# Expert weights of a mixture-of-experts decoder step: 12 loads of 1 MB per expert become 6 of 2 MB, with strided transposes

## The reference

```
logits = x @ router_w + router_b                      # 32 experts, top 4 per token
gate   = softmax(top 4 logits)
for each expert e, for its tokens:
    h      = x @ w_gu[e] + b_gu[e]                    # 1024 -> 2048
    hg, hu = h[:, :1024], h[:, 1024:]
    act    = (clip(hu, -7, 7) + 1) * min(hg, 7) * sigmoid(1.702 * min(hg, 7))
    y     += gate * (act @ w_down[e] + b_down[e])     # 1024 -> 1024
```

## Time and profile before

| | us |
|---|---|
| median of 3 runs (1538.61 to 1538.96) | 1538.8 |
| the profiled execution | 1540.0 |
| its span, first to last instruction | 1538.0 |
| TensorE busy (9323 matmuls) | 1448.0 |
| VectorE busy | 523.0 |
| ScalarE busy | 287.9 |

### The profile page before, as it was taken

One profiled execution on the slowest core, in us unless ns is written; L12 is line 12 of the kernel. 1 busy time (PEld: TensorE's weight loads), 2 busy tenths in 40 slices (PEclk: granted clock), 3 DMA queues, 4 the chain that ended last, 5 costly groups with the idle time before them and its releaser, 6 DMA issues.

```text
span 1538.0 us, 24574 instructions
## 1 busy us (share of the span) xinstructions
PE 1448.0 (94%) x9323; PEld 684.9 (45%) x9323; DVE 523.0 (34%) x1106; ACT 287.9 (19%) x501; POOL 107.4 (7%) x174
## 2 busy tenths in 40 slices
PE   6978899999999989999999999999999999999995
PEld 4755568866665633333333333333333333333332
DVE  6877665442321142321321322312131223122223
ACT  3111331212213321111111111111111111111111
POOL 1189600000000000000000000000000000000000
PEclk9998899997999989999999999999999999999997
DMA  7853111012658549999999999999999999999991
GB/s 308 178 126 56 52 62 57 30 57 100 272 206 363 202 158 418 417 419 418 416 418 419 418 416 418 419 417 418 418 418 416 418 419 418 417 418 419 416 383 46
DMA packets 86697, 471.61 MB, mean 307 GB/s; under 512 B 7986, under 2 KB 13234, under 8 KB 46964
## 3 DMA queue, kind: packets, MB, share of 16 engines
q1 hardware_dynamic: 80356, 460.90, 74.0%
q10 hardware_dynamic: 6288, 9.95, 3.3%
HBM read 465.08 MB, written 5.74 MB: 306 GB/s over the span
## 4 chain that ended last, share of the span: by engine, by line
PE 60%; DMA 15%; SPq 13%; DVE 5%; issue 4%; ACT 2%; DVEq 0%; ACTq 0%
DMA big<-in_w_gu 15%; PE bank L1009 14%; SPq L529 10%; PE bank L586 10%; PE bank L1039 10%; PE bank L959 4%; SPq L515 3%; PE bank L669 2%; PE bank L1058 2%; PE bank L839 2%; PE bank L763 1%; PE bank L965 1%; PE bank L973 1%; ACT big L1293 1%; PE bank L755 1%
## 5 line engine op out<-in xcount | busy, mean ns | idle before, releaser
L1009 PE MATMUL bank<-big 128*64 128x512 f32 x2048 | 456.0, 597 | 16.3 <-DMA big<-in_w_gu 16.3
L1009 PEld LDWEIGHTS bank<-big 128*64 128x64 f32 x2048 | 141.2, 137 | 317.2 <-issue 257.8
L1039 PE MATMUL bank<-big 128*64 128x512 f32 x1024 | 226.8, 595 | 0.0
L1851 DVE TENSOR_TENSOR big<-big,bank 128x320 f32<-128x320 f32 x256 | 104.7, 483 | 355.1 <-PE bank L1058 355.1
L586 PE MATMUL bank<-big 128*128 128x320 f32 (+1 forms) x688 | 189.0, 434 | 2.3 <-ACT big L1238 1.3
L586 PEld LDWEIGHTS bank<-big 128*128 128x128 f32 x688 | 132.7, 194 | 57.9 <-issue 6.5
L1837 DVE TENSOR_SCALAR big<-bank 128x512 f32<-128x512 f32 x32 | 22.2, 693 | 331.5 <-PE bank L1009 331.5
L1039 PEld LDWEIGHTS bank<-big 128*64 128x64 f32 x1024 | 70.8, 137 | 133.2 <-issue 127.8
L1307 ACT ACTIVATE big<-big 128x512 f32<-128x512 f32 x32 | 20.3, 633 | 525.1 <-DVE big L1837 525.1
L1091 ACT ACTIVATE big<-bank 128x320 f32<-128x320 f32 (+3 forms) x122 | 53.2, 436 | 250.4 <-PE bank L586 59.1
L959 PE MATMUL bank<-big 128*64 128x512 f32 x396 | 94.2, 611 | 0.2 <-issue 0.2
(11 more groups left out here) (357 smaller groups left out, 1217.7 us busy)
## 6 DMA issues: line engine op xcount, KB each, us to landing
big<-in_w_gu SPq DMA_DIRECT2D x256, 1024.0 KB, 18.9
big<-in_w_down SPq DMA_DIRECT2D x128, 1024.0 KB, 21.9
big<-in_dense SPq DMA_DIRECT2D x47, 1024.0 KB, 7.9
big<-u_windows ACTq DMA_DIRECT2D x32, 160.0 KB, 7.3
out_y<-big SPq DMA_DIRECT2D x3, 512.0 KB, 2.7
big<-in_smw SPq DMA_DIRECT2D x1, 1408.0 KB, 19.4
big<-in_xT SPq DMA_DIRECT2D x2, 640.0 KB, 4.6
big<-in_b_gu SPq DMA_DIRECT2D x66, 4.0 KB
```

What stands on the lines that cost most here:

```text
L1009: last = mm(ps[bank][part, :], xte[:, k, :], w[:, at:at + 512], start=False, stop=(k == KT - 1))
L1039: last = mm(ps[4][part, :], actT[:, k % 4, (k // 4) * CAP:(k // 4 + 1) * CAP], w[:, k % 2, s * 512:s * 512 + 512], start=(k == 0), stop=(k ...
L1851: tt(part, part, ps[bank][:, 0:T], add).then_inc(psum_free[bank], 1)
```

## The change

Two chunks become one load. Load j (0 to 3) of `w_gu` takes 256 consecutive rows, and partition p gets rows 2p and 2p+1 of them, 16 KB that are consecutive in memory. Load 4 or 5, of `w_down`, takes 512 rows, and partition p gets rows 4p to 4p+3, 16 KB too. The slots are the same, taken in neighbouring pairs. Since a partition now holds rows 2p and 2p+1 instead of p and 128 + p, the transposes read every second column of `hrow` and every fourth of `hact`, so that the contraction meets the right rows. TensorE waits once per load, and tells SyncE once per load that it is used (`load_used`).

```diff
@@ -111,6 +111,10 @@
 USES = [SLOT.count(s) for s in range(SLOTS)]
 NTH = [SLOT[:c].count(SLOT[c]) for c in range(NPRE)]
 EXPERT_CHUNKS = 12
+LOADS = EXPERT_CHUNKS // 2
+LOAD_SLOT = [EXPERT_SLOT[2 * j] for j in range(LOADS)]
+LOAD_AT = [CHUNK * min(EXPERT_SLOT[2 * j:2 * j + 2]) for j in range(LOADS)]
+assert all(abs(EXPERT_SLOT[2 * j] - EXPERT_SLOT[2 * j + 1]) == 1 for j in range(LOADS))
 
 
 class Regions:
@@ -490,17 +494,16 @@
                 sp.dma_start(view(SLOT[c] * CHUNK, CHUNK), a["dense"][c]).then_inc(ring_full[SLOT[c]], 16)
 
 
-            def expert_chunk(j, e):
-                return a["w_gu"][e, j * P:(j + 1) * P, :] if j < 8 else \
-                    a["w_down"][e, (j - 8) * 2 * P:(j - 7) * 2 * P, :].rearrange("(i p) n -> p i n", i=2)
-
-            def expert_dst(j):
-                at = EXPERT_SLOT[j] * CHUNK
-                return view(at, CHUNK) if j < 8 else view(at, 2, D)
-
-            for j in range(EXPERT_CHUNKS):
-                computed(sp, LAST_JOB[NPRE - EXPERT_CHUNKS + j])
-                sp.dma_start(expert_dst(j), expert_chunk(j, 0)).then_inc(ring_full[EXPERT_SLOT[j]], 16)
+            def load(j, e):
+
+                src = a["w_gu"][e, j * 2 * P:(j + 1) * 2 * P, :].rearrange("(p i) n -> p (i n)", i=2) if j < 4 else \
+                    a["w_down"][e, (j - 4) * 4 * P:(j - 3) * 4 * P, :].rearrange("(p i) n -> p (i n)", i=4)
+                sp.dma_start(view(LOAD_AT[j], 2 * CHUNK), src).then_inc(ring_full[LOAD_SLOT[j]], 16)
+
+            for j in range(LOADS):
+                for c in range(2):
+                    computed(sp, LAST_JOB[NPRE - EXPERT_CHUNKS + 2 * j + c])
+                load(j, 0)
             computed(sp, "co7")
             for r in range(4):
                 sp.dma_start(BIG[32 * r:32 * r + 32, BDOWN:BDOWN + 2 * P], a["b_down"][:, r * 2 * P:(r + 1) * 2 * P]).then_inc(S("bdown_in"), 16)
@@ -519,14 +522,14 @@
 
             def load_expert(it, e):
 
-                for j in range(EXPERT_CHUNKS):
-                    if j == 7:
+                for j in range(LOADS):
+                    if j == 3:
                         sp.wait_ge(psum_full[1], it + BANK_USES[1])
-                    elif j == 11:
+                    elif j == 5:
                         sp.wait_ge(psum_full[4], it * 2 + (BANK_USES[4] - 1))
                     else:
-                        sp.wait_ge(S("chunk_used"), it * 10 + ((j if j < 7 else j - 1) - 9))
-                    sp.dma_start(expert_dst(j), expert_chunk(j, e)).then_inc(ring_full[EXPERT_SLOT[j]], 16)
+                        sp.wait_ge(S("load_used"), it * 4 + ((j if j < 3 else 3) - 3))
+                    load(j, e)
                 load_bias(it, e)
 
             with sp.Fori(1, NE) as e:
@@ -961,8 +964,9 @@
 
             def gathered():
 
+                pairs = hrow.rearrange("p (j c i) -> p j i c", j=2, i=2)
                 for k in range(4):
-                    last = nc.tensor.transpose(ps[2][:, k * P:(k + 1) * P], hrow[:, k * P:(k + 1) * P], ident)
+                    last = nc.tensor.transpose(ps[2][:, k * P:(k + 1) * P], pairs[:, k // 2, k % 2], ident)
                 last.then_inc(psum_full[2], 1)
 
             def start_bias():
@@ -1000,17 +1004,18 @@
 
                 pe.wait_ge(S("xte_copied"), it + 1)
                 for k in range(KT):
-                    slot = EXPERT_SLOT[k]
-                    pe.wait_ge(ring_full[slot], it * 16 + 16 * (USES[slot] + 1))
-                    w = view(slot * CHUNK, CHUNK)
+                    j = k // 2
+                    if k % 2 == 0:
+                        pe.wait_ge(ring_full[LOAD_SLOT[j]], it * 16 + 16 * (USES[LOAD_SLOT[j]] + 1))
+                    w = view(LOAD_AT[j] + k % 2 * CHUNK, CHUNK)
                     for bank in (0, 1):
                         for s, part in sides:
                             at = bank * FF + s * 512
                             last = mm(ps[bank][part, :], xte[:, k, :], w[:, at:at + 512], start=False, stop=(k == KT - 1))
                         if k == KT - 1:
                             last.then_inc(psum_full[bank], 1)
-                    if k < KT - 1:
-                        last.then_inc(S("chunk_used"), 1)
+                    if k % 2 and k < KT - 1:
+                        last.then_inc(S("load_used"), 1)
 
                 pe.wait_ge(psum_free[5], it * 2 + BANK_USES[5])
                 pe.wait_ge(S("weighted"), it + 1)
@@ -1022,8 +1027,9 @@
                 gather()
                 pe.wait_ge(psum_free[3], it * 2 + BANK_USES[3])
                 pe.wait_ge(S("activated"), it + 1)
+                quads = hact.rearrange("p (c i) -> p i c", i=4)
                 for k in range(4):
-                    last = nc.tensor.transpose(ps[3][:, k * P:(k + 1) * P], hact[:, k * P:(k + 1) * P], ident)
+                    last = nc.tensor.transpose(ps[3][:, k * P:(k + 1) * P], quads[:, k], ident)
                 last.then_inc(psum_full[3], 1)
 
                 pe.wait_ge(psum_free[2], it * 2 + (BANK_USES[2] + 2))
@@ -1031,17 +1037,17 @@
                 pe.wait_ge(psum_free[3], it * 2 + (BANK_USES[3] + 1))
                 pe.wait_ge(psum_free[4], it * 2 + BANK_USES[4])
                 for k in range(KT):
-                    slot = EXPERT_SLOT[8 + k // 2]
-                    if k % 2 == 0:
-                        pe.wait_ge(ring_full[slot], it * 16 + 16 * (USES[slot] + 1))
-                    w = view(slot * CHUNK, 2, D)
+                    j = 4 + k // 4
+                    if k % 4 == 0:
+                        pe.wait_ge(ring_full[LOAD_SLOT[j]], it * 16 + 16 * (USES[LOAD_SLOT[j]] + 1))
+                    w = view(LOAD_AT[j], 4, D)
                     for s, part in sides:
-                        last = mm(ps[4][part, :], actT[:, k % 4, (k // 4) * CAP:(k // 4 + 1) * CAP], w[:, k % 2, s * 512:s * 512 + 512],
+                        last = mm(ps[4][part, :], actT[:, k % 4, (k // 4) * CAP:(k // 4 + 1) * CAP], w[:, k % 4, s * 512:s * 512 + 512],
                                   start=(k == 0), stop=(k == KT - 1))
                     if k == KT - 1:
                         last.then_inc(psum_full[4], 1)
-                    elif k % 2:
-                        last.then_inc(S("chunk_used"), 1)
+                    elif k == 3:
+                        last.then_inc(S("load_used"), 1)
                 for bank in (0, 1):
                     pe.wait_ge(psum_free[bank], it + (BANK_USES[bank] + 1))
                 pe.wait_ge(S("bias_in"), it * 32 + 64)
```

## The result

The changed kernel takes **1521.05 us** (median of 4 runs, 1521.02 to 1522.36), the kernel before beside it on the same chip 1538.88 (4 runs, 1538.61 to 1541.33): ratio 0.9883, 95% interval 0.9869 to 0.9897. The prediction was 1522.0, range 1513.5 to 1536.0. The profiled execution took 1521.05 us with a span of 1519.0, 19.0 less than the span of before; the medians are 17.8 apart.

The account below looks back on a forecast made before the run. TensorE's matmuls were taken to bound early experts and DMA the late ones, 24.1 us of waiting. Packets and pairing left 7.3, gaining 16.8; strides and small things cost 0: 1540.0 to 1523.2 profiled, median 1522.0, range 1513.5 to 1536.0.

Parts of the forecast that it names:

- the lead: Weight loads ahead of TensorE: 16.0 us at expert 1 before the change, shrinking 1.35 per expert, lasting 12 experts.
- the 24.1 us: Waiting for DMA on `w_gu` loads in the kernel before; the most that changing the loads alone could bring.
- The two bias rows: Two 4 KB loads per expert, assumed to go to one DMA engine, explaining 0.3 us of the late period.
- Part 1: Weight loads in 16 KB packets: 616 ns each, 0.68 us less per expert, late period 29.76 us.
- the middle of the two slopes: Price of a 16 KB packet: 616 ns, between extrapolations of 613.3 (4 to 8 KB) and 618.3 (8,192 to 11,264 B).
- rival 1: TensorE bounds every expert, packets 611 ns or less: all 24.1 us come back, 1514.7 us; chance 0.12.
- Part 2: Paired loads and slots: lead 12.8 us, lasting 19 experts, last load 7.3 us late; gain 16.8 us.
- Part 3: Strided weight loads of the `hact` and `hrow` transposes: taken as costing nothing, at most 0.42 us per group.
- Rival 2: Strided weight loads cost TensorE: `hact` doubled 0.42 us per expert, 1528.1 (chance 0.13); both groups, 1538.7 (0.06).
- Part 4: Fewer SyncE issues and TensorE waits, later router bias before the experts: cost 0, bias at most 0.5 us.
- 3: Rival on weight packets: length gives nothing above 8 KB, 623.4 ns, 6.1 us gained, 1532.7 us; chance 0.12.
- 4: Rival on weight loads: 16 KB runs move worse, slower beyond 627.5 ns per packet, deeper grain costing 3.2 us lead; chance 0.12.

Follow-up runs that it names:

- 1: Kernel before with paired 2 MB loads, but its old rows per partition (8 and 4 KB packets) and unstrided transposes: 1544.26 us, ratio 1.0036.
- experiment 2: Changed kernel with 12 loads of one chunk each, 8 KB consecutive per partition: 1531.24 us, ratio 0.9954.
- experiment 5: Kernel before with all bias rows loaded once ahead of the experts, VectorE picking each expert's row: 1529.15 us, ratio 0.9935.
- experiment 6: Changed kernel with all bias rows loaded once ahead of the experts, VectorE picking each expert's row: 1519.47 us, ratio 0.9869.
- experiment 3: Changed kernel with transposes reading consecutive columns again, so rows don't match the weights: 1520.71 us, ratio 0.9887.
- 8: Changed kernel with bias rows loaded once and `hact` permuted in VectorE's write; `hrow` transposes still strided: 1520.06 us, ratio 0.9873.
- 10: Changed kernel with bias rows loaded once and token rows written permuted ahead of the experts, freeing only `hrow`: 1521.24 us, ratio 0.9886.
- 12: Changed kernel with bias rows loaded once and both `hact` and token rows written permuted, so no transpose is strided: 1518.62 us, ratio 0.9860.

## Why the prediction was right, and where it wasn't

**The bound, the lead, the 24.1 us** stood. Two regimes, the wait at the late one, and the packet length as its price are shown by experiments 1 and 2, which came 2.3 and 1.2 us above what was expected.

**The two bias rows** ("I take it that both go to one of the 16 DMA engines") were an assumption and are now shown by 5: 0.32 us per expert, 0.3 assumed. The prediction only carried them along; that they were the cheapest thing to remove it didn't see.

**Part 1.** Predicted 616 ns per packet, 29.76 us per expert; measured 611 to 612 and 29.69. The step mis-sized is "the middle of the two slopes". From the pace of the landings (29.37 us of a fast engine per expert, 48 packets; 29.82 in experiment 2, 96 packets; 30.12 before) a packet costs 160.1, 310.6 and 611.8 ns: each further 4 KB costs the same 150.5 ns, the slope from 4 to 8 KB. The slope from 8,192 to 11,264 B was the wrong one, and the counts gave 311.7 where the landings give 310.6, so that even the low end, 613.3, came out too high. That the period is off by only 0.07 is partly luck. At 612 ns its own sum would give 29.57, but it also took 30.25 us for an engine's share before where the landings give 30.12, 0.13 too much; the two errors cancel in part. (The costs per packet are estimates from the landings of before, after and 2, over 18 experts each.) The Trainium skill (DMA: Bandwidth & Descriptors, "Why small descriptors are slow") gave an estimated 606 ns; the trace is 5 to 6 above it, as it was 7 above for 8 KB. What kept the kernel from rival 1 were, by experiment 6, the two bias rows.

**Part 2.** The lead was put at 12.8 us. Load 3 of expert 1 landed at 587.1 and was needed at 600.4: 13.3. It lasted 27 experts, not 19, since it shrank by 29.69 - 29.175 = 0.52 per expert and not 0.67. The last load came 1.7 us late (landing 1477.37, needed at 590.02 + 10.41 + 30 x 29.175 = 1475.7), not 7.3. With TensorE's own 30 x 0.085 = 2.6 us, 4.3 of the 24.1 stayed and 19.8 came back, where 16.8 was predicted.

**Part 3** is the step that failed. "I take nothing" was wrong: 70 ns a load, 0.085 us per expert. By the prediction's own sign, "I am wrong if the early period isn't 29.09", it failed here: the early period is 29.175. It was cheap by luck of place: a group of four takes 0.75 for 0.66 us, since matmuls and loads run at the same time (both from 869.68 in the timeline above), and while DMA set the end the loss was hidden (3). "L1026 is on the path: what it costs comes through whole" is half of it. It is on the path and `hrow`'s L969 is beside it, equally long; 8, 10 and 12 show both. With only the one strided the period is the same 29.17. Rival 2 is thus right in kind, a fifth of its size (0.085 for 0.42). The rule weighed there (the Trainium skill, SBUF — State Buffer, "Door 1: The DMA port swizzle") says 8 B steps are free and 16 B steps at the edge. These traces agree for weight loads at 16 B, 209 ns against 139, and disagree at 8 B, where it is 208. The measurement decides.

**Part 4** priced the start too low. The router bias cost about 0.2 us of the 0.5 allowed, by a landing of 8.6 for 5.7 us, and the eaten lead was the 2.7 us named; but from the logits' transposes to the second expert it took 2.1 us longer, and 2.0 to 2.5 in every execution profiled with paired loads and the bias rows as before. What brings the part beyond the bias stays open. The issues and waits of SyncE and TensorE cost nothing in the loop: with them and without the strides, experiment 3 has 29.09 early, as before.

**The sum** gave 16.8 us less, and the profiled executions are 19.0 apart: 3.0 more came back in the loop and 1.3 in the tail, 2.6 were lost ahead of it, which leaves 0.5 that these terms don't account for. The medians, 17.8 apart, are 1.0 us from what was predicted. That is partly luck: the loop's 3.0 are the change's, so are some 2 of the 2.6, and they nearly cancel; the tail's 1.3 go with the granted clock, which no step of the prediction counted.

**Rivals.** 1 (TensorE bounds all, 1514.7) was nearly there in the periods, 27 of 31, and with the bias rows gone, all; in the time it was 6.4 us off, since TensorE's own period was longer and the start later. 3 (no gain from length) is excluded by 2 against after: 422 to 429 GB/s. 4's mechanism, the loss of lead by the grain, is what 1 isolates: 2.8 us in the loop, for the 3.2 named, in a median 5.5 us slower.

## What to carry to other kernels

Longer runs per partition and larger loads are two changes with opposite signs: length raises the rate, size shortens the lead; price them apart. When every load waits for all DMA engines, count what goes to one of them alone: 8 KB per expert cost 9 to 10 us here, and splitting it was worse than removing it. And before calling an instruction "the one on the path", look for a second branch that ends at the same moment: two equal branches hide each other in every experiment that frees only one. And read the stretch ahead of a loop too: pairing the loads lost some 2 us there, and the copies that freed the second branch cost as much there as they gave in the loop.

## What the runs showed of the hardware

- A 128x128 fp32 weight load took 139 ns from consecutive columns and 208 to 209 with steps of 8 or 16 B from element to element.
- Permuting in the write instead, neighbours going 512 B apart: ScalarE's 128x512 copy from 0.60 to 1.06 us, VectorE's product from 0.69 to 1.07.
- A DMA engine took 160 to 161, 311 to 312 and 611 to 612 ns per packet of 4, 8 and 16 KB: about 25.5, 26.3 and 26.8 GB/s. By the landings each further 4 KB cost 150.5 ns.
- With two 4 KB rows per expert loaded, one DMA engine fell behind the other fifteen by 0.32 us per expert; without them (experiment 5) all sixteen finished within 1.0 us.
- Thirty-two packets of 256 B per expert into two partitions cost more than two of 4 KB, 30.56 for 30.44 us late; why is open.
- After a pause of 6.5 us in the tail, the same 32 matmuls ran at a granted clock of 0.53 in one execution and 0.69 in the other, means of the 1.2 and 2.4 GHz levels, and took 1.3 us longer in the first.
